# A fused transformer block on one core: norm factor applied after the projection, first two units side by side, no barrier ahead of the mixer loop, fewer column sums

## The reference, cut to what matters

```python
h = rmsnorm(x, norm1_w)              # x * rsqrt(mean(x*x) + EPS) * w, one factor per token
proj = h @ w_in                      # 1024 x 3592
qkv_a, z_a, b_a, a_a, qkv_b = ...    # 1536, 512, 4, 4 and 1536 columns
qkv_a = silu(causal_dwconv(qkv_a, conv_qkv_w))       # 4 taps
qa, ka = l2norm(qa) * 128 ** -0.5, l2norm(ka)        # v is not normalised
o_a = rmsnorm(gated_delta_rule(qa, ka, va, g, beta), gdn_norm_w) * silu(z)
o_b = dilated_attention(qb, kb, vb)
x = x + concat(o_a, o_b) @ w_out     # then a feed-forward layer, a second block, a final norm
```

## Time and profile before

| | us |
|---|---|
| median of 3 runs | 2598.08 |
| lowest and highest of them | 2595.64, 2599.38 |
| the profiled execution, whole | 2599.83 |
| its span, first to last instruction | 2598.2 |

### The profile page before, as it was taken

The page is one execution under the profiler, slowest core; times in us unless marked ns, Lnnn a source line. Parts: engine busy times, 40 slices in busy tenths (PEclk is TensorE's granted clock), DMA queues, the critical chain, the costliest instruction groups (busy, mean ns, idle before and its releaser), DMA issues.

```text
span 2598.2 us, 35525 instructions
## 1 busy us (share of the span) xinstructions
PE 2498.2 (96%) x13930; PEld 2040.9 (79%) x13930; DVE 1492.2 (57%) x2457; ACT 1105.3 (43%) x1779; POOL 67.2 (3%) x118
## 2 busy tenths in 40 slices
PE   6999997999899999999999999889999999999997
PEld 4878875778788788887788888777888788888886
DVE  4114325666446666656658954465788756655555
ACT  3123334676735344445544553444343434433332
POOL 1000000000000000000000000000000000000000
PEclk9999998999999999999999999989999999999999
DMA  5322213111054555565534554423332232333331
GB/s 191 98 81 81 81 65 102 59 59 35 13 182 154 162 193 191 195 205 176 167 98 153 188 184 135 143 65 104 90 92 89 89 98 89 114 109 97 96 97 64
DMA packets 318466, 304.29 MB, mean 117 GB/s; under 512 B 10223, under 2 KB 277860, under 8 KB 318180
## 3 DMA queue, kind: packets, MB, share of 16 engines
q1 hardware_dynamic: 303332, 243.92, 31.2%
q0 software_dynamic: 14976, 58.20, 5.5%
HBM read 244.41 MB, written 57.67 MB: 116 GB/s over the span
## 4 chain that ended last, share of the span: by engine, by line
PE 85%; DVE 7%; ACT 3%; issue 3%; DMA 2%; SPq 0%; POOLq 0%; POOL 0%; DVEq 0%; ACTq 0%
PE PS L2021 13%; PE PS L2023 13%; PE PS L2022 13%; PE PS L1727 12%; PE PS L2038 7%; PE PS L2039 7%; PE PS L2040 7%; PE PS L1852 3%; PE PS L1838 1%; PE PS L1980 1%; PE PS L1956 1%; PE PS L1968 1%; DVE wl L1284 1%; DVE cg L1674 1%; ACT wh L941 1%
## 5 line engine op out<-in xcount | busy, mean ns | idle before, releaser
L2021 PE MATMUL PS<-hh,wh 128*128 128x512 f32 x1728 | 683.8, 396 | 2.3 <-DVE hl L1543 1.6
L2023 PE MATMUL PS<-hh,wl 128*128 128x512 f32 x1728 | 673.8, 390 | 0.0
L2022 PE MATMUL PS<-hl,wh 128*128 128x512 f32 x1728 | 673.6, 390 | 0.0
L941 ACT ACTIVATE wh<-raw 128x1024 fp32r<-128x1024 f32 x352 | 366.8, 1055 | 514.2 <-PE PS L2040 381.5
L1284 DVE TENSOR_TENSOR wl<-raw,wh 128x1024 fp32r<-128x1024 f32 x286 | 347.7, 1228 | 390.7 <-ACT wh L941 390.5
L1570 DVE TENSOR_TENSOR x<-x,PS 128x512 f32<-128x512 f32 x432 | 294.1, 686 | 183.2 <-PE PS L2040 182.4
L2021 PEld LDWEIGHTS PS<-hh,wh 128*128 128x128 f32 x1728 | 325.2, 188 | 74.4 <-issue 4.8
L2022 PEld LDWEIGHTS PS<-hl,wh 128*128 128x128 f32 x1728 | 325.3, 188 | 70.9 <-issue 4.6
L2023 PEld LDWEIGHTS PS<-hh,wl 128*128 128x128 f32 x1728 | 325.0, 188 | 68.2
L2038 PE MATMUL PS<-fh,wh 128*128 128x512 f32 x864 | 344.6, 399 | 18.6 <-DVE x L1570 10.8
L2039 PE MATMUL PS<-fl,wh 128*128 128x512 f32 x864 | 340.0, 394 | 0.0
(11 more groups left out here) (293 smaller groups left out, 2531.3 us busy)
## 6 DMA issues: line engine op xcount, KB each, us to landing
raw<-in_w_ff SPq DMA_DIRECT2D x128, 512.0 KB, 3.9
raw<-in_w_up SPq DMA_DIRECT2D x88, 512.0 KB, 4.4
wl_s<-wl POOLq DMA_DIRECT2D x66, 512.0 KB, 5.4
wl<-wl_s SPq DMA_DIRECT2D x66, 512.0 KB, 3.5
raw<-in_w_in SPq DMA_DIRECT2D x60, 512.0 KB, 3.9
raw<-in_w_down SPq DMA_DIRECT2D x44, 512.0 KB, 5.0
raw<-in_w_out SPq DMA_DIRECT2D x32, 512.0 KB, 4.1
qkvz_s<-st POOLq DMA_DIRECT2D x16, 512.0 KB, 2.9
```

What stands on the lines that cost most here:

```text
L941: A(whs(slot), raw[:, k % 2], ACT.Copy).then_inc(s["w_hi"], 1)
L2021: mm(bank, wh[:, k % 4, cut], hh[:, kk, span(a_)], start=kk == 0, stop=False)
L2022: mm(bank, wh[:, k % 4, cut], hl[:, kk, span(a_)], start=False, stop=False)
L2023: last = mm(bank, wl[:, k % 4, cut], hh[:, kk, span(a_)], start=False, stop=kk == KT - 1)
```

## The change

- **Order of the front.** ACT, no longer SP, starts the load of x. SP loads the first unit's weights ahead of the gains, the second unit's behind them. `hh` is now the rounded x * gain, without the factor (ACT, `high`), and `hl` the rest (DVE, `low`). POOL takes no part. PE transposes tiles 0 and 1 of x as they land, two more, and then alternates: the products wh·hh and wl·hh of tile k for units 0 and 1, and the transpose of tile k+4. The factors are spread afterwards and copied to SBUF (`Rb`). Then follow the products wh·hl of both units. Squares go to SBUF.
- **The factor on the products.** Each unit's products are multiplied by `Rb` on DVE once the unit is done (`by_token_scale`), in PSUM, or for z into `sqb`. ACT waits for that.
- **Column sums** are taken for q and k alone. The placeholder square and its wait are gone.
- **b and a**: high and low weights lie side by side as 16 columns, so two products are needed per tile and half instead of three. DVE adds the two halves afterwards.
- **No barrier ahead of the mixer loop.** Its buffers are laid out anew, so that the first chunk, the first pair and the tables can be loaded while units still run. The three Exp stand ahead of the last Silu. The loop's first PE work waits for the last scaling, the first `ttr` for the stores of z.
- The loops over `U_QKV` are unrolled.

Cut to its core (eight columns of indentation are taken off):

```diff
 small = sb("small", [P, 256])
-bah, bal, baw = sb("bah", [P, 8, 8], F32R), sb("bal", [P, 8, 8], F32R), sb("baw", [P, 8, 8])
+bahl, baw = sb("bahl", [P, 8, 16], F32R), sb("baw", [P, 8, 8])
+bah, bal = bahl[:, :, 0:8], bahl[:, :, 8:16]
...
+    ch = sb("ch", [P, 2, 16, P], where=z)
+    qkvb = [sb("qkvb0", [P, 3, S], where=z)]
+    lmask = sb("lmask", [P, LEVELS - 1, 64], where=z)
     neg, identc = sb("neg", [P, P], where=z), sb("identc", [P, 64], where=z)
-    ch = sb("ch", [P, 2, 16, P], where=z)
...
         dst = raw[:, k % 2] if down else raw[:, k % 2].rearrange("p (k n) -> p k n", k=KT)
         sp.dma_start(dst, src).then_inc(w_loaded[k % 2], 16)
-    for i in range(4):
-        sp.dma_start(xin[:, 2 * i:2 * i + 2], a["x"][0].rearrange("(t p) d -> p t d", p=P)[:, 2 * i:2 * i + 2])\
-            .then_inc(tile_moved[i], 16)
-    for dst, src in ((ident, a["c_ident"]), (triu, a["c_triu"])):
-        sp.dma_start(dst[:], src).then_inc(s["const_loaded"], 16)
+    sp.dma_start(ident[:], a["c_ident"]).then_inc(s["const_loaded"], 16)
+    load(U_QKVB, cols(w_in, 2056))
     n = 0
     for name, lo in (("norm1_w", C_N1), ("norm2_w", C_N2), ("final_norm_w", C_NF), ("norm1_g_2", C_M1),
...
+    for n in range(2):
+        load(U_Z + n, cols(w_in, 1536 + P * n))
+    sp.wait_ge(s["x_spilled"], 16)
+    sp.wait_ge(s["st_written"], U_QKV + 1)
+    for b in range(4):
+        sp.wait_ge(st_free[b], 48)
     sp.dma_start(neg[:], a["c_after"]).then_inc(s["tables_loaded"], 16)
-    pair(0)
     sp.dma_start(strip[:], a["c_strip"]).then_inc(s["tables_loaded"], 16)
     sp.dma_start(lmask[:], a["c_levels"]).then_inc(s["tables_loaded"], 16)
-    chunk(1)
+    pair(0)
+    for n in range(2, 4):
+        load(U_Z + n, cols(w_in, 1536 + P * n))
+    for b in range(4):
+        sp.wait_ge(st_free[b], 96)
+    for c in range(2):
+        sp.dma_start(ch[:, c, 0:12], qkvz_s[:, 0:12, c * P:(c + 1) * P]).then_inc(ch_loaded[c], 16)
+    for n in range(2):
+        load(U_OUT1 + n, cols(w_out, P * n))
+    for b in range(4):
+        sp.wait_ge(st_free[b], 112)
     pair(1)
+    for c in range(2):
+        sp.dma_start(ch[:, c, 12:16], qkvz_s[:, 12:16, c * P:(c + 1) * P]).then_inc(s["z_loaded"], 16)
     for c in range(2, TT):
         chunk(c)
         if c in (3, 5):
             pair((c + 1) // 2)
...
+    def square(t):
         act.wait_ge(tile_moved[t // 2], 16)
         if t:
             act.wait_ge(s["n_sq"], t)
-        A(acc(3), xin[:, t], ACT.Square, accum_out=small[:, 200 + t:201 + t]).then_inc(s["n_sq"], 1)
-    norm_root(0)
+        A(sqt[:, t % 2], xin[:, t], ACT.Square, accum_out=small[:, 200 + t:201 + t]).then_inc(s["n_sq"], 1)
...
+            act.wait_ge(s["x_written"], max(k, 1))
+        A(hh[:, k], x[:, k], ACT.Copy, scale=par[:, C_N1 + k:C_N1 + k + 1]).then_inc(s["n_hi"], 1)
+    for i in range(4):
+        act.dma_start(xin[:, 2 * i:2 * i + 2], a["x"][0].rearrange("(t p) d -> p t d", p=P)[:, 2 * i:2 * i + 2])\
+            .then_inc(tile_moved[i], 16)
+    square(0)
+    square(1)
...
+    square(2)
+    square(3)
+    square(4)
+    square(5)
     prep(1, 1)
+    act.wait_ge(s["xt_mm"], 2)
+    A(x[:, 1], acc(3), ACT.Copy).then_inc(s["x_one"], 1)
+    act.wait_ge(s["par_ready"], 4)
+    for k in range(3):
+        high(k)
+    square(6)
+    high(3)
+    high(4)
+    square(7)
+    high(5)
+    act.wait_ge(s["n_v"], 1)
+    A(small[:, 16:24], small[:, 8:16], ACT.Sqrt).then_inc(s["n_sd"], 1)
+    high(6)
+    high(7)
     act.wait_ge(s["ba_loaded"], 16)
-    A(bah[:], baw[:], ACT.Copy).then_inc(s["ba_hi"], 1)
+    A(bah, baw[:], ACT.Copy).then_inc(s["ba_hi"], 1)
     for n in range(12):
         prep(n + 2, (n + 2) % 4)
-        act.wait_ge(s["w_used"], n + 1)
...
-    with act.Fori(0, 3) as i:
+    for i in range(3):
         for u in range(4):
             prep(U_QKV + u + 2, (u + 2) % 4, 4, i)
-            act.wait_ge(s["w_used"], U_QKV + u + 1 + 4 * i)
+            act.wait_ge(s["scaled"], U_QKV + u + 1 + 4 * i)
...
-            act.wait_ge(s["col_mm"], 4 * i + u + 1)
-            A(sqb[:], st[:, u], ACT.Square).then_inc(s["st_written"], 1)
-    act.wait_ge(s["ba_mm"], 1)
-    A(cacc[0:8, 1, :], acc(2)[0:8], ACT.Copy).then_inc(s["ba_copied"], 1)
+            if i < 2:
...
+        if n == 3:
+            act.wait_ge(s["tab_dve"], 4)
+            for dst, src, sign in ((T_NGAM, T_NGC, -1.0), (T_GE, T_GE, 1.0), (T_KE, T_KE, 1.0)):
+                A(tab[:, :, dst:dst + 4], tab[:, :, src:src + 4], ACT.Exp, scale=sign).then_inc(s["tab_act"], 1)
+        act.wait_ge(s["scaled"], U_Z + n + 2)
         act.wait_ge(st_free[n], 96)
-        A(st[:, n], acc(n % 2), ACT.Silu).then_inc(s["st_written"], 1)
+        A(st[:, n], sqb[:], ACT.Silu).then_inc(s["st_written"], 1)
         if n == 0:
             act.wait_ge(s["rows_loaded"], 32)
...
-    for dst, src, sign in ((T_NGAM, T_NGC, -1.0), (T_GE, T_GE, 1.0), (T_KE, T_KE, 1.0)):
-        A(tab[:, :, dst:dst + 4], tab[:, :, src:src + 4], ACT.Exp, scale=sign).then_inc(s["tab_act"], 1)
-    end_phase(act, 1)
     for stage in mixers.order["act"]:
...
-        dve.wait_ge(s["n_sd"], r + 1)
+    def copy(k):
+        dve.wait_ge(s["xt_mm"], k + 1)
+        V_.tensor_copy(x[:, k], acc(2 + k % 2)).then_inc(s["x_written"], 1)
+    def low(k):
+        dve.wait_ge(s["n_hi"], k + 1)
+        STT(hl[:, k], x[:, k], par[:, C_N1 + k:C_N1 + k + 1], hh[:, k].bitcast(F32),
+            ALU.mult, ALU.subtract).then_inc(s["n_lo"], 1)
...
+    def by_token_scale(dst, src, k):
+        dve.wait_ge(s["w_used"], k)
+        TTo(dst, src, Rb[:], ALU.mult).then_inc(s["scaled"], 1)
...
     prep(0, 0)
+    prep(1, 1)
+    copy(0)
+    copy(2)
+    copy(3)
+    low(0)
+    copy(4)
+    low(1)
+    copy(5)
+    copy(6)
+    low(2)
+    copy(7)
+    norm_mean()
+    low(3)
+    norm_diagonal()
+    low(4)
+    low(5)
...
+    V_.tensor_copy(Rb[:], acc(3)).then_inc(s["r_copied"], 1)
+    low(6)
+    low(7)
...
-    with dve.Fori(0, 3) as i:
+        by_token_scale(acc(n % 2), acc(n % 2), n + 1)
+    for i in range(3):
         for u in range(4):
             prep(U_QKV + u + 2, (u + 2) % 4, 4, i)
+            by_token_scale(acc(u % 2), acc(u % 2), U_QKV + 4 * i + u + 1)
...
+    dve.wait_ge(s["ba_mm"], 1)
+    TTo(acc(2)[0:16], acc(2)[0:16], Rb[0:16], ALU.mult).then_inc(s["scaled"], 1)
     prep(U_Z + 2, 2)
-    dve.wait_ge(s["silu"], 12)
-    dve.wait_ge(s["col_mm"], 12)
+    dve.wait_ge(s["st_written"], U_Z)
+    dve.wait_ge(s["col_mm"], 8)
+    by_token_scale(sqb[:], acc(0), U_Z + 1)
...
     prep(U_Z + 3, 3)
-    for n in range(2):
-        prep(U_OUT1 + n, n)
+    dve.wait_ge(s["st_written"], U_Z + 1)
+    by_token_scale(sqb[:], acc(1), U_Z + 2)
+    prep(U_OUT1, 0)
+    dve.wait_ge(s["st_written"], U_Z + 2)
...
+    prep(U_OUT1 + 1, 1)
+    dve.wait_ge(s["st_written"], U_Z + 3)
+    by_token_scale(sqb[:], acc(1), U_Z + 4)
     dve.wait_ge(s["tables_loaded"], 48)
...
         elif name == "og":
             dve.wait_ge(s["ot_mm"], c + 1)
...
             dve.wait_ge(s["s_mm"], step(c, j, m) + 1)
+            if c == 0 and (j, m, e) == (0, 0, 0):
+                for b in range(4):
...
+    pe.wait_ge(s["par_ready"], 4)
     for k in range(KT):
-        if k >= 2:
-            pe.wait_ge(s["x_written"], k - 1)
-        for t in range(TT):
-            last = tr(acc(k % 2)[:, t * P:(t + 1) * P], xin[:, t, k * P:(k + 1) * P], ident[:])
...
-    pe.wait_ge(s["par_ready"], 4)
-    norm_factor(0)
-    for n in range(12):
-        if n >= 2:
-            pe.wait_ge(s["st_written"], n - 1)
-        unit(n, n % 4, n % 2, stats=0 if n == 0 else None)
-    pe.wait_ge(s["sq_init"], 1)
-    with pe.Fori(0, 3) as i:
+    pe.wait_ge(s["n_diag"], 1)
+    pe.wait_ge(s["x_written"], KT - 1)
+    for t in range(2):
+        last = mm(acc(3)[:, t * HALF:(t + 1) * HALF], ones[:], diag[:, 4 * t:4 * t + 4, :], start=True, stop=True)
+    last.then_inc(s["n_R"], 1)
+    for k in range(KT):
...
+        for n in range(2):
+            last = both_halves(n, whs(n), hl, k, stop=k == KT - 1)
+            if k == KT - 1:
+                last.then_inc(s["w_used"], 1)
+    for n in range(2, 12):
+        pe.wait_ge(s["st_written"], n - 1)
+        unit(n, n % 4, n % 2)
+    for i in range(3):
         for u in range(4):
             pe.wait_ge(s["st_written"], 11 + 4 * i + u)
             unit(U_QKV + u, u, u % 2, 4, i)
-            pe.wait_ge(s["st_written"], 12 + 4 * i + u)
-            for tt in range(TT):
-                last = mm(PS[:, 7, bass.ds(tt * 12 + 4 * i + u, 1)], sqb[:, tt * P:(tt + 1) * P], ones[:, 0:1],
-                          start=True, stop=True)
-            last.then_inc(s["col_mm"], 1)
+            if 0 < 4 * i + u <= 8:
+                pe.wait_ge(s["st_written"], 12 + 4 * i + u)
+                for tt in range(TT):
+                    last = mm(PS[:, 7, bass.ds(tt * 12 + 4 * i + u, 1)], sqb[:, tt * P:(tt + 1) * P], ones[:, 0:1],
+                              start=True, stop=True)
```

(8 more changed lines are left out.)

238 lines of the change are left out of this document (105 added, 133 removed).

## The result

The changed kernel takes 2561.01 us (median of 4 runs, 2560.07 to 2561.68). The kernel before, run beside it, takes 2598.72 (2595.64 to 2599.38). The ratio is 0.9856, with a 95% interval of 0.9844 to 0.9867: 37.7 us less, where the prediction said 45.4 less. The direction was right and the stated range, 2545 to 2566, holds the time.

The account below looks back on a forecast made before the run. PE, busy 96% of the span, was taken as the bound; gains of 14.9 + 2.5 + 6.7 + 3.7 + 17.6 = 45.4 us brought the median 2598.08 to 2552.7, stated as 2553, range 2545 to 2566.

Parts of the forecast that it names:

- Column sums: Between units on PE: four of twelve column sums go, at 1.68 us each, gain 6.7 us.
- b and a: On PE: 32 of 48 matmuls remain for b and a, at 0.232 us each, gain 3.7 us.
- Scaling at zero: In U_QKV: DVE's scaling passes, 1.28 us each, stay hidden under a cover of 1.5 and 0.9 us; cost zero.
- Ahead of U_QKV, 2.5: Ahead of U_QKV: PE's wait goes with the placeholder square, gain 2.5 us.
- Rival C: Front and U_QKV: x isn't delayed (1.9 us) and unrolling saves 0.1 to 0.15 us per unit (1.8); total 2549, chance 0.11.
- Start of the loop, 17.6: From the last unit's end to the mixer loop's first `ttr`: 7.3 us instead of 24.9, gain 17.6, bounds 14 to 18.5.
- Rival B: Start of the mixer loop: an early load or z's store is late after all; gain there 5.7, total 2565, chance 0.09.
- The front, 14.9: Kernel start up to unit 2: unit 2 starts at 51.2 us instead of 66.1, gain 14.9, bounds 8 to 17.
- Rival A: Front: gains land late and PE starts at the 1.2 GHz level; gain 8 instead of 14.9, total 2560, chance 0.17.
- The signs that I gave for the stretch behind the copy: Front: a PE gap of about 2 us ahead of unit 2, hardly one between 18 and 49 us.
- the low end: Whole kernel: rival C with the bounds 17 (front) and 18.5 (loop's start), 2547.7, less 2.4 for the fastest run: 2545.

Follow-up runs that it names:

- p_extra2: The changed kernel with two more in-place DVE passes over each unit of U_QKV; 2563.87 us, 2.9 above the changed kernel.
- b_square: The kernel before, with ACT's placeholder square made behind the fourth unit instead of the twelfth; 2593.82 us against 2598.73, ratio 0.9982.
- l_late: The changed kernel, without barrier, but with the mixer loop's loads issued behind the projection's last store; 2578.79 us, 17.8 above the changed kernel.
- l_barrier: The changed kernel with the barrier back ahead of the mixer loop and the loop's loads left ahead of it; 2569.22 us, 8.2 above the changed kernel.
- f_order: The changed kernel with loads untouched and work reordered on PE, DVE and ACT in the front; 2555.84 us, 5.2 below the changed kernel.

## Why the prediction was right, and where it was off

- **Column sums, b and a.** 1.68 each and 7.41: as forecast, 6.7 and 3.7.
- **Scaling at zero.** Right. The pass took 1.23 (1.28 taken), and the cover was deeper than counted (p_extra2).
- **Ahead of U_QKV, 2.5.** Mis-sized: 4.1 by b_square. The row with unit 12 at 12.53 stood in the earlier trace rows beside units of 11.05, and I read only the gap ahead of it.
- **Rival C's unrolled loop.** It gives nothing: a unit of U_QKV right behind a column sum takes 11.05 unrolled as in the loop before, and 10.88 where no sum stands ahead of it. So the extra 0.15 to 0.17 belongs to the sum. Three more units have none ahead of them now, which is the other 0.5 of the 2.2 from unit 2 to E.
- **Start of the loop, 17.6.** Right in size (17.7) and mechanism; l_late and l_barrier show that it took both halves of the edit. Rival B (one of the loads late after all) did not come: no load ends a wait on the chain between E and `ttr`. Of the drain that the Trainium skill (ScalarE: Activation LUTs, "What ACT_TABLE_LOAD costs") counts with a table load the traces here show nothing: in l_barrier the load takes 375.76 to 377.04 and the Exp starts at 377.05.
- **The front, 14.9.** Here lies the miss (8.2 between the two traces). The step that failed is "tile 0 is ready at 16.5 and its copy, behind a weight split on DVE, at about 18.3". The copy ended at 24.94. x was not late: where PE took it at once (f_order) it had landed at 15.60, my 15.6. But I had counted one weight split ahead of that copy, and the code has four more things there: DVE's copies of the gains into `par`, which wait for the gains; a second split; ACT's four squares between the two splits; and PE's transposes of the gains ahead of those of x. Rival A named the gains, and its size came out (gain 8, 2560 in total), but it put the rest on PE's clock. The slow stretch in the changed kernel (27.4 to 29.8) cost only 0.8 more than I had counted (the first 8 matmuls took 2.67 us instead of 1.8), and the order of the engines, which rival A does not name, the rest. So that its figure came true is in good part luck. The order was the larger part: with the loads untouched f_order starts unit 2 at 51.46, where I had 51.2. Even so its front falls 2.1 short of mine at the mark, since I let unit 2 take 10.9 and with slow pairs behind the wait it takes 12.8. The gains "landed before x" was wrong as well (18.6, and 15.57 even when first in the queue). The signs that I gave for the stretch behind the copy all came: from 24.98 on PE waits for no `hh` or `hl`, and a gap of 1.93 stands ahead of unit 2.
- **The Trainium skill** (DMA: Bandwidth & Descriptors, "Issuing engines are not separate DMA queues") says that transfers of different issuers run on the same DMA engines and interleave. The traces agree: in f_order, whose loads are those of the changed kernel, the last of x is there at 15.60, 1.9 later than in the earlier trace rows, and in the changed kernel the weight load beside it took 14.55 us. I weighed the rule for x alone, and not for what would pay more, the weights and the gains.
- **The rest.** From `ttr` to the end 1.4 us were lost, in a part whose work the change leaves as it was. The same stretch takes 2185.7 in the kernel before and in b_square, and 2185.1 to 2187.2 in the ten other variants of the changed kernel. So 1.4 is within what this stretch varies by from trace to trace; which rows make it up was not found. The last column sums, 1.07 us before (at 2582.34) and 1.85 after, look like a part of it, but they take 1.88 in b_square, whose stretch is as short as that of before. The other 1.7 us lie between the profiled runs (39.35 apart) and the medians (37.7 apart): the profiled run of before, 2599.83, took longer than any of the four behind its median, and its front is 3.6 longer than that of b_square.
- **A slip in the sum of the low end.** Rival C with both bounds comes to 2547.9, not 2547.7. It changes nothing.

In all: 45.4 forecast, less 6.7 in the front, plus 2.2 between unit 2 and E, plus 0.1 at the loop's start gives the 41.0 us at `ttr`; less 1.4 at the end, 0.25 outside the span and 1.7 for the median gives the 37.7. The front's 6.7 holds for these two traces; measured from b_square's front, the miss there would be 10.3.
